# A decoder layer with a new front: modulation rows by column quadrants from four buffers, input rows and weights split inside the front, two products begun there

## The reference, cut to what matters

```
mod = c @ ada_w + ada_b                      # (1 + 8 rows) x 6144
sh1, sc1, g1, sh2, sc2, g2 = split(mod, 6)
h   = layer_norm(x) * (1 + sc1) + sh1        # 520 rows x 1024
proj = h @ w_in                              # r | k | v | decay-lora, iclr-lora | gate-lora | pool | gates
prev = state_shift @ w_in[:, :D_SHIFT]       # 8 more rows, the samples' previous token
xs  = cur + (prev_rows - cur) * mu_shift     # token shift on r, k, v and the loras
```

## Time and profile before

| what | before |
| --- | --- |
| median of 3 runs | 1241.78 us |
| the profiled execution | 1242.95 us |
| its span, first to last instruction | 1241.2 us |
| granted TensorE clock, mean | 0.971 |
| busy: PE, PEld, DVE, ACT, POOL | 1133.0, 1033.3, 701.4, 487.3, 100.3 us |
| second block begins (first weight load issued) | 74.77 us |
| product 3 begins on PE | 107.56 us |

### The profile page before, as it was taken

One profiled execution on the slowest core, in us unless ns is written; L12 is line 12 of the kernel. 1 busy time (PEld: TensorE's weight loads), 2 busy tenths in 40 slices (PEclk: granted clock), 3 DMA queues, 4 the chain that ended last, 5 costly groups with the idle time before them and its releaser, 6 DMA issues.

```text
span 1241.2 us, 34809 instructions
## 1 busy us (share of the span) xinstructions
PE 1133.0 (91%) x15404; PEld 1033.3 (83%) x15404; DVE 701.4 (57%) x1131; ACT 487.3 (39%) x800; POOL 100.3 (8%) x152
## 2 busy tenths in 40 slices
PE   3968899999999999999999999789999999699995
PEld 1357788888888887899998999689989998689995
DVE  2134666667757666368913645947576757632336
ACT  0235535345344452363333333563535344422221
POOL 0000311203203112000000000500000000000000
PEclk9969999999999999999999999899999999989998
DMA  8330220210202211058875632132222222343221
GB/s 265 140 91 18 58 59 4 59 41 21 60 3 59 59 37 55 21 181 232 238 221 170 221 104 69 70 102 86 84 84 85 84 84 81 102 128 93 83 68 69
DMA packets 186176, 117.50 MB, mean 95 GB/s; under 512 B 6484, under 2 KB 177290, under 8 KB 185889
## 3 DMA queue, kind: packets, MB, share of 16 engines
q1 hardware_dynamic: 155889, 100.37, 27.0%
q10 hardware_dynamic: 30160, 15.21, 4.5%
HBM read 108.40 MB, written 7.34 MB: 93 GB/s over the span
## 4 chain that ended last, share of the span: by engine, by line
PE 31%; issue 8%; DVE 8%; ACT 6%; DMA 1%; POOL 1%; DVEq 1%; ACTq 0%; POOLq 0%
PE PJ L231 23%; PE PJ L223 4%; ACT ACC L1841 2%; ACT Wh L1647 2%; DVE ACC L2241 2%; DVE ACC L2242 1%; DVE ACC L2249 1%; DMA AD<-in_ada_w_dram 1%; DVE ACC L2247 1%; PE BB L1416 1%; ACT ACC L1839 1%; DVE Wl L1891 1%; PE BB L231 0%; ACT SFh L1848 0%; PE BB L223 0%
## 5 line engine op out<-in xcount | busy, mean ns | idle before, releaser
L231 PE MATMUL PJ<-Hh,Wh 128*128 128x260 f32 (+1 forms) x1184 | 264.2, 304 | 28.5 <-DVE Wl L1891 13.4
L231 PE MATMUL PJ<-Hh,Wl 128*128 128x260 f32 (+1 forms) x1184 | 240.3, 284 | 1.5 <-issue 1.5
L231 PE MATMUL PJ<-Hl,Wh 128*128 128x260 f32 (+1 forms) x1184 | 241.1, 285 | 0.0
L231 PEld LDWEIGHTS PJ<-Hh,Wh 128*128 128x128 f32 x1184 | 184.8, 190 | 51.5 <-issue 32.1
L231 PEld LDWEIGHTS PJ<-Hh,Wl 128*128 128x128 f32 x1184 | 185.1, 190 | 1.7 <-issue 1.7
L231 PEld LDWEIGHTS PJ<-Hl,Wh 128*128 128x128 f32 x1184 | 184.9, 190 | 0.0
L1891 DVE TENSOR_TENSOR Wl<-RAW,Wh 128x1024 fp32r<-128x1024 f32 (+2 forms) x102 | 118.1, 1161 | 108.6 <-ACT Wh L1647 103.2
L1647 ACT ACTIVATE Wh<-RAW 128x1024 fp32r<-128x1024 f32 (+2 forms) x106 | 106.8, 1010 | 121.0 <-PE PJ L231 116.9
L2241 DVE SCALAR_TENSOR_TENSOR ACC<-ACC,CP 128x512 f32<-128x512 f32 x88 | 66.0, 750 | 71.4 <-ACT ACC L1841 69.8
L1207 POOL TENSOR_TENSOR MO<-BP,CST 128x512 f32<-128x512 f32 x40 | 55.8, 1401 | 310.9 <-DVE KP L1085 251.6
L231 PE MATMUL PJ<-SFh,Wh 128*128 128x256 f32 (+1 forms) x308 | 64.6, 292 | 13.4 <-DVE Wl L1891 13.4
(11 more groups left out here) (372 smaller groups left out, 2174.7 us busy)
## 6 DMA issues: line engine op xcount, KB each, us to landing
RAW<-in_w_in_dram SPq DMA_DIRECT2D x46, 512.0 KB, 5.0
RAW<-in_ffn_up_dram SPq DMA_DIRECT2D x44, 512.0 KB, 3.8
AD<-in_ada_w_dram ACTq DMA_DIRECT2D x19, 512.0 KB, 5.9
RAW<-in_ffn_down_dram SPq DMA_DIRECT2D x16, 512.0 KB, 4.0
RAW<-in_ada_w_dram ACTq DMA_DIRECT2D x10, 512.0 KB, 5.4
RAW<-in_ada_w_dram SPq DMA_DIRECT2D x2, 2048.0 KB, 10.5
ACC<-in_ada_w_dram SPq DMA_DIRECT2D x2, 2048.0 KB, 13.1
RAW<-in_w_branch_rwkv_dram SPq DMA_DIRECT2D x8, 512.0 KB, 4.1
```

Of the source, the lines that this page charges most:

```text
L231: mm = pe.matmul(out[:, b, 0:nb[b]], w[:, slot, kw, :], x[:, kx, c0:c0 + nb[b]], start=first and w is Wh and x is xh, stop=last and w is Wl)
```

## The change: what it does

- Loads: SP issues only the 128 columns of the identity first, then c, the first half of x, the samples, the pool and convolution states, the second half of x, and quarters 0 and 2 of `ada_w`. The 15 parameter loads, the last columns of the constants and `state_shift` are issued by ACT. Quarter 1 goes as two halves over `Wh` and `Wl` slots 2 and 3, quarter 3 over `SC0` once that has been transposed (`st_in`), so no quarter waits for another one's buffer. When the first rows are done SP also issues the weights of products 0 and 1 inside the front, and later those of 2, 3 and 4, and the rest of the constants.
- Modulation rows: `rows` puts channel tile k in column quadrant k mod 4 of the array (`tile_position`), 32 columns of `CT` each; the four partial sums are added by `turn`, now four 128-row matmuls with the selector `sel`. The quarters are taken in the order 0, 2, 1, 3: shift and scale of channel tiles 0 to 3, then of 4 to 7.
- Input: states are transposed first and evicted by ACT. x is transposed before the modulation is ready; ACT (even k) and DVE (odd k) evict it plain, and DVE applies scale and shift in SBUF (`full`), as each half of the modulation arrives. `Hh` and `Hl` are made per channel tile behind it.
- Products 0 and 1 run in the front, k = 0 to 3 after the first two quarters and k = 4 to 7 after the other two. Products 2 and 3 take the four `BB` banks in the second block, so 2 waits for no read and 3 for no `alpha`. Weights 0, 1 and 2 are split in the front.
- The new shift rows use `BB` and run after the second halves.
- `mod_rows`, `t_x`, `hl_b`, `hfd`, `nb` and `hf` counts that later blocks use are offset (`past`); their instructions stay.

The diff, cut to its core:

```diff
+            ORDER = (0, 2, 1, 3)
+            AW0 = RAW[:].rearrange("p a k d -> p (a k d)").rearrange("p (k d) -> p k d", k=KT)
+            AW1 = [place("AW1", [P, KT, 2 * P], "Wh", 2 * D), place("AW2", [P, KT, 2 * P], "Wl", 2 * D)]
+            AW2 = ACC[:, 0:4 * KT * P].rearrange("p (k d) -> p k d", k=KT)
+            AW3 = place("AW3", [P, KT, 4 * P], "SC0")
+            def ada_part(c):
+                return {0: [AW0], 1: [AW1[0][:], AW1[1][:]], 2: [AW2], 3: [AW3[:]]}[c]
+            def ada_src(c, a, n):
+                return wsrc["ada"][:, :, 4 * P * c + a:4 * P * c + a + n]
+            SMPL = PJ[0][:, 1, 0:KT * NS].rearrange("p (a b) -> p a b", a=KT)
+            STAT = PJ[0][:, 1, KT * NS:2 * KT * NS].rearrange("p (a b) -> p a b", a=KT)
...
-                sp.dma_start(CST[:], i["consts"]).then_inc(S("ld_cst"), 16)
+                sp.dma_start(CST[:, C_ID:C_ID + P], i["consts"][:, C_ID:C_ID + P]).then_inc(S("ld_id"), 16)
                 sp.dma_start(CT0[0:1, :], i["c_prompt"]).then_inc(S("ld_c"), 16)
                 sp.dma_start(CT0[1:NMOD, :], i["c_sample"]).then_inc(S("ld_c"), 16)
-                g0 = [("mu_shift", R_MU, 24, 0), ("decay_w0", R_W0, 8, 0), ("aaa_a0", R_A0, 8, 0), ("k_k", R_KK, 8, 0),
...
-                sp.dma_start(XT[:, 0:4, :], i["x_prompt"][0].rearrange("(a p) d -> p a d", p=P)).then_inc(S("ld_x"), 16)
+                x = i["x_prompt"][0].rearrange("(a p) d -> p a d", p=P)
+                sp.dma_start(XT[:, 0:2, :], x[:, 0:2, :]).then_inc(S("ld_x"), 16)
                 sp.dma_start(XT[0:NS, 4, :], i["x_sample"][:, 0, :]).then_inc(S("ld_x"), 16)
-                for b in range(2):
-                    sp.dma_start(AW[b], ada_src(b)).then_inc(S(f"ld_ada{b}"), 16)
-                sp.dma_start(SH0[:], i["state_shift"][0]).then_inc(S("ld_st"), 16)
                 sp.dma_start(SP0[:], i["state_pool"][0].rearrange("b t d -> (b t) d")).then_inc(S("ld_st"), 16)
                 sp.dma_start(SC0[:], i["state_conv"][0].rearrange("b t d -> (b t) d")).then_inc(S("ld_st"), 16)
+                sp.dma_start(XT[:, 2:4, :], x[:, 2:4, :]).then_inc(S("ld_x2"), 16)
+                sp.dma_start(AW0, ada_src(0, 0, 4 * P)).then_inc(S("ld_ada0"), 16)
+                sp.dma_start(AW2, ada_src(2, 0, 4 * P)).then_inc(S("ld_ada1"), 16)
+                sp.wait_ge(S("ada_used"), 1)
+                for q in range(2):
+                    sp.dma_start(RAW[:, q], cols("in", 24 + q)).then_inc(S(f"w_load{q}"), 16)
+                for a in range(2):
+                    sp.dma_start(AW1[a][:], ada_src(1, 2 * P * a, 2 * P)).then_inc(S("ld_ada2"), 16)
+                sp.wait_ge(S("st_in"), 1)
+                sp.dma_start(AW3[:], ada_src(3, 0, 4 * P)).then_inc(S("ld_ada3"), 16)
+                sp.dma_start(RAW[:, 2], cols("in", KT)).then_inc(S("w_load2"), 16)
+                sp.dma_start(CST[:, P:C_EPS], i["consts"][:, P:C_EPS]).then_inc(S("ld_id"), 16)
                 sp.dma_start(o["pool_s"][0, :, 0:PB - 1, :], i["state_pool"][0, :, 1:PB, :]).then_inc(S("out"), 16)
                 sp.dma_start(o["conv_s"][0, :, 0, :], i["state_conv"][0, :, 1, :]).then_inc(S("out"), 16)
-                for b in range(2):
-                    sp.wait_ge(S("ada_used"), b + 1)
-                    sp.dma_start(AW[b], ada_src(2 + b)).then_inc(S(f"ld_ada{b}"), 16)
+                for q in range(2):
+                    w_load(sp, B_RKV + 1 + q, q, cols("in", 2 * KT * q))
                 sp.wait_ge(S("sho"), 1)
                 sp.dma_start(o["shift_p"][0], SHO[0:1, :]).then_inc(S("out"), 16)
                 sp.dma_start(o["shift_s"][0], SHO[1:NMOD, :]).then_inc(S("out"), 16)
+                sp.wait_ge(S("ld_id"), 32)
...
+                def rows(o_):
+                    c = ORDER[o_]
+                    pe.wait_ge(S(("ld_ada0", "ld_ada2", "ld_ada1", "ld_ada3")[c]), 32 if c == 1 else 16)
+                    after(pe, "mod_rows", o_)
+                    parts = ada_part(c)
+                    w = 4 * P // len(parts)
+                    for a, src in enumerate(parts):
+                        for k in range(KT):
+                            g = k % 4
+                            mm = pe.matmul(B[2][32 * g:32 * g + 32, w * a:w * a + w], CT[:, k, :], src[:, k, :], start=k < 4, stop=k >= 4,
+                                           tile_position=(0, 32 * g))
+                    mm.then_inc(S("ada_used"), 1)
+                def turn(o_):
+                    pe.wait_ge(S("mod_rows"), o_ + 1)
+                    after(pe, "mod", o_)
+                    for s in range(4):
+                        mm = pe.matmul(B[3][:, s * NMOD:(s + 1) * NMOD], MR[:, o_ % 2, s * P:(s + 1) * P], sel, start=True, stop=True)
+                    mm.then_inc(S("t_mod"), 1)
+                def project(n, k0):
+                    pe.wait_ge(S("w_lo"), n + 1)
+                    for k in range(k0, k0 + 4):
+                        pe.wait_ge(S("hl_b"), k + 1)
+                        mm = kstep(pe, PJ[n], n, k, Hh, Hl, k, k == 0, k == KT - 1, (260, 268))
+                    if k0 > 0:
+                        mm.then_inc(S("prj"), 1)
+                pe.wait_ge(S("ld_cst"), 16)
+                rows(0)
+                pe.wait_ge(S("xn"), 5)
+                for k in range(KT):
+                    after(pe, "xo" if k % 2 else "xe", k // 2)
+                    for t in range(4):
+                        mm = pe.transpose(B[k % 2][:, t * P:(t + 1) * P], XN[:, t, k * P:(k + 1) * P], ident)
+                    mm.then_inc(S("t_x"), 1)
+                pe.wait_ge(S("ld_st"), 48)
+                for k in range(KT):
+                    mm = pe.transpose(SMPL[:, k, :], XN[0:NS, 4, k * P:(k + 1) * P], ident[0:NS, 0:NS])
+                    mm = pe.transpose(STAT[:, k, :], SH0[:, k * P:(k + 1) * P], ident[0:NS, 0:NS])
+                mm.then_inc(S("t_s"), 1)
+                rows(1)
+                turn(0)
+                turn(1)
                 pe.wait_ge(S("st_in"), 1)
+                pe.wait_ge(S("hfd"), 1)
+                project(0, 0)
+                project(1, 0)
+                rows(2)
+                turn(2)
+                rows(3)
+                turn(3)
+                project(0, 4)
+                project(1, 4)
+                pe.wait_ge(S("hfd"), 5)
...
+                act.dma_start(CST[:, C_EPS:C_END], i["consts"][:, C_EPS:C_END]).then_inc(S("ld_cst"), 16)
+                act.dma_start(SH0[:], i["state_shift"][0]).then_inc(S("ld_st"), 16)
...
+                act.wait_ge(S("t_st"), 1)
+                for g in range(NPOOL):
+                    act.activation(PLS[:, g, 0:PB, :].rearrange("p t b -> p b t"),
+                                   PJ[0][:, 0, g * P:g * P + NS * PB].rearrange("p (b t) -> p b t", b=NS), ACT.Copy)
+                for b in range(2):
+                    st = act.activation(SCV[:, 22 * b:22 * b + 22].rearrange("p f b t -> p f (b t)"),
+                                        PJ[1][:, b, 0:352].rearrange("p (f b) -> p f b", f=22), ACT.Copy)
+                st.then_inc(S("st_in"), 1)
...
+                mod_rows(0)
+                for k in range(0, KT, 2):
                     act.wait_ge(S("t_x"), k + 1)
-                    act.activation(Hf[:, k, 0:T], B[k % 2], ACT.Identity, bias=MOD[:, k, 0:1],
-                                   scale=MOD[:, KT + k, 0:1]).then_inc(S("hf"), 1)
-                for k in range(KT):
-                    act.wait_ge(S("hf"), KT + 1)
-                    act.activation(Hh[:, k, :], Hf[:, k, :], ACT.Copy).then_inc(S("hh"), 1)
+                    act.activation(Hf[:, k, 0:T], B[0], ACT.Copy).then_inc(S("xe"), 1)
+                mod_rows(1)
+                split(0)
+                for k in range(4):
+                    high(k)
+                    if k == 0:
+                        split(1)
+                mod_rows(2)
+                mod_rows(3)
+                for k in range(4, KT):
+                    high(k)
+                split(2)
...
+                dve.wait_ge(S("ld_x"), 32)
+                dve.wait_ge(S("chain"), 1)
+                for t in (0, 1):
+                    stats(t)
+                dve.wait_ge(S("nb"), 2)
+                join(0)
+                join(1)
...
+                for k in range(1, KT, 2):
+                    dve.wait_ge(S("t_x"), k + 1)
+                    dve.tensor_copy(Hf[:, k, 0:T], B[1]).then_inc(S("xo"), 1)
...
+                def full(k):
+                    after(dve, "xe", k // 2 + 1)
+                    dve.tensor_scalar(Hf[:, k, 0:T], Hf[:, k, 0:T], MOD[:, KT + k, 0:1], MOD[:, k, 0:1], ALU.mult, ALU.add).then_inc(S("hf"), 1)
...
+                for h in range(2):
+                    modulation(2 * h)
+                    modulation(2 * h + 1)
+                    sample(h)
+                    if h == 0:
+                        dve.wait_ge(S("xo"), 4)
+                    full(4 * h)
+                    full(4 * h + 1)
+                    if h == 0:
+                        lo(0)
```

(30 more changed lines are left out.)

204 lines of the change are left out of this document (86 added, 118 removed).

## The result

The changed kernel takes 1222.62 us, the median of four runs (1221.37 to 1223.75), against 1241.49 (1239.45 to 1242.0) for the kernel before beside it: the ratio is 0.9842, 95% interval 0.9816 to 0.9868. Timed once more later, it was 1220.26 us, ratio 0.9828 (0.9801 to 0.9856). The forecast was 1216.0 with a range of 1209 to 1227: direction and range held, the size came out a quarter smaller (18.9 us of 25.5).

A forecast was written before the change was run, and what follows sets the result against it. PE's product stream was taken as the bound, so the gain is its earlier start: product 3 at 81.7 instead of 107.56 us, 25.9 off the 1241.2 span, 1215.3; profiled 1217.1, median 1216, range 1209 to 1227.

The forecast's parts named there:

- x normalised: Front, before x's transposes: normalising takes 3.7 us behind the root at 20.4, ending at 24.5.
- at 0.35 each 6.6 us, plus 3.4 to land, 10.0: Start of the front: ACT issues 17 loads at 0.35 us each, and they have landed by 10.0 us.
- rival A: ACT's loads are held behind SP's backlog or issue slowly; parameters at 18 to 26 us, time 1224 to 1230; chance 0.10.
- bounds of 9 to 26 us: Landing of ACT's loads in the front, if one issue takes 0.30 or 1.30 us; 0.35 was taken.
- x's transposes and their copies: Front, after normalising: 8 groups of 4 transposes evicted by two engines, 6.3 to 7.6 us, taken as 7.
- A change of tiling mode: Between quadrant rows and products: a possible 0.3 us drain at each of eight changes, 2.4 us, left inside the range.
- The second block's part: From the second block's start at 70.1 to product 3 at 81.7: a chain of ACT and DVE, 11.6 us.
- The last premise: Behind product 3: the order of work is as before, so the rest shifts with it, by 25.9 us.
- C: Front quicker than forecast: PE warm throughout, faster evictions and x transposes, 5 to 7 us, 1209 to 1211; chance 0.15.
- D: Slower than before: the low clock lasts past product 3 through the first head pair into the second, 1245; chance 0.03.
- E: The front gives nothing on: something else binds the stream's start at about 105 us, 1241; chance 0.02.
- B: PE's clock stays low through the front, lengthening rows, turns, product 1 and second halves: 1223 to 1226; chance 0.15.

The follow-up runs named there:

- p2: Changed kernel with SP's queue held until ACT's 15 parameter loads have landed, before the convolution state, second half of x and modulation weights are issued: 1217.25 us.
- a0: The changed kernel run and profiled once more with nothing edited: 1220.26 us.
- p1: Changed kernel with one load moved, the convolution state issued behind the second half of x instead of ahead of it: 1220.91 us.

## Why the prediction was right, and where its size was off

Its own steps against the changed kernel's profile, in us:

| step | forecast | measured | late by |
|---|---|---|---|
| first half of x reaches DVE | 7.8 | 7.63 | -0.2 |
| ACT's loads landed (parameters / states) | 10.0 | 16.35 / 18.17 | 6.4 / 8.2 |
| states transposed | 16.4 | 24.0 | 7.6 |
| root taken | 20.4 | 27.4 | 7.0 |
| x normalised | 24.5 | 31.3 | 6.8 |
| first matmul of product 0 | 41.0 | 47.4 | 6.4 |
| last turn ends | 56.4 | 62.5 | 6.1 |
| second halves end | 67.2 | 74.0 | 6.8 |
| second block begins | 70.1 | 77.05 | 7.0 |
| product 3 begins | 81.7 | 86.98 | 5.3 |

The mechanism was right: PE's stream was moved as a whole, and what moved it was the front. The 6.6 us by which the forecast of 1216.0 was too low are 5.3 at product 3 and 1.3 lost behind it. One term was mis-sized, *"at 0.35 each 6.6 us, plus 3.4 to land, 10.0"*. The issuing was right, 0.28 to 0.64 us each, the last one at 7.3; the 3.4 to land came from rows in which a load had the DMA engines to itself or stood ahead of the others in the same queue. Its effect is rival A's, and A had the wrong place: *"If ACT's issuing stands behind SP's backlog"* does not happen. The bounds of 9 to 26 us held the truth, 18.2; the value taken was near the low end. The large loads were late as well, which the other lateness hid: quarter 0 landed at about 21.5 us instead of 17.4, quarter 2 at 26.8 instead of 22.6. p2 is the check on the parameters alone: with them at 10.09, product 3 begins at 82.67, 1.0 us from the forecast, and the time is 1217.25, 1.2 from it. That it comes so near is in part luck. In p2 the states still wait for the convolution state until 15.15 and are transposed at 21.0, 4.6 us late, the second block begins 2.6 late, and the rest is made up in it.

The sum has one slip: a root taken at 20.4 and 3.7 of normalising give 24.1, where it has 24.5.

From there on the steps kept their lengths within 1 us, with errors that cancel. Rows of a quarter 1.93 at full clock (1.8 forecast); x's transposes and their copies 7.2 (7); a full turn 1.06 (0.95); second halves 8.8 (8.2), at the lower clock until 71.2, where half and half was assumed. A change of tiling mode cost 0.1 us at most where it can be read: quarter 2's rows begin at 55.11, 0.34 us behind the start of the last pair of product matmuls, where such pairs follow each other in 0.24. The drain that the Trainium skill names ("TensorEngine Tiling (Array Packing)", "Tiling Modes") may be that, and eight of them would not make the 2.4 us that were weighed.

The second block's part took 9.9 us, not 11.6: ACT's three steps were added one behind the other with their waits from before, but weights and products were there, so ACT ran through them with hardly a gap, and `lora(0, 0)` to product 3 took 1.5 instead of 2.6 (85.46 to 86.98).

The last premise, that the stream keeps its length, held to 517 us, where the lead was 21.4, and failed after it, at 19.4 by 792 us. That is mostly the wandering clock and waits, not the change: a0 and p1, with product 3 0.2 and 0.8 us later, ended with spans of 1218.7 and 1218.5. The kernel before was profiled only once, so its own length wanders unseen.

Of the rivals, C, D and E did not occur; B only in part: the granted clock was 0.85 from 40 to 65 us and 0.74 from 65 to 77.
